# Attention in a two-block layer stack: values become the stationary operand, and the softmax reciprocals are transposed instead of the results

## What is computed

```
p = softmax(logits, axis=-1)                     # per head, 128 queries x 128 or 256 keys
o = einsum("bhqs,bshd->bqhd", p, v)              # head width 64
y = g_a * (o_sparse @ w_branch_a) + g_b * (o_fox @ w_branch_b)
```

## Time and profile before

| | |
|---|---|
| three runs | 1537.84, 1539.54, 1540.49 us (median 1539.54) |
| profiled execution, first to last instruction (its span) | 1539.0 us |
| instructions | 31311 |
| TensorE clock granted, mean | 0.991 of full speed |
| DMA | 290.51 MB, mean 189 GB/s |

### The profile page before, as it was taken

The page is one execution under the profiler, slowest core; times in us unless marked ns, Lnnn a source line. Parts: engine busy times, 40 slices in busy tenths (PEclk is TensorE's granted clock), DMA queues, the critical chain, the costliest instruction groups (busy, mean ns, idle before and its releaser), DMA issues.

```text
span 1539.0 us, 31311 instructions
## 1 busy us (share of the span) xinstructions
PE 1495.4 (97%) x12608; PEld 1433.2 (93%) x12608; DVE 1144.0 (74%) x2202; ACT 833.0 (54%) x1509; POOL 31.2 (2%) x36
## 2 busy tenths in 40 slices
PE   5999999999998999999999999999999999999997
PEld 3898998999997999989999999999999999999997
DVE  5758566888645587668987678878966988888774
ACT  3655545655434556446665565645455754645453
POOL 0000001000000000010001000000000000000000
PEclk8999999999999999999999999999999999999998
DMA  9655555567776452354555543443446444444430
GB/s 397 247 205 194 204 222 219 217 254 271 274 271 251 166 205 97 144 185 142 188 190 197 212 172 118 174 176 138 159 151 243 155 152 161 168 161 144 168 129 29
DMA packets 48128, 290.51 MB, mean 189 GB/s; under 512 B 10024, under 2 KB 12328, under 8 KB 13424
## 3 DMA queue, kind: packets, MB, share of 16 engines
q1 hardware_dynamic: 39168, 280.83, 48.7%
q10 hardware_dynamic: 8816, 7.67, 1.5%
HBM read 286.09 MB, written 2.39 MB: 187 GB/s over the span
## 4 chain that ended last, share of the span: by engine, by line
PE 57%; DVE 1%; ACT 1%; DMA 0%; issue 0%; DVEq 0%; ACTq 0%
PE bank L1371 17%; PE bank L1377 16%; PE bank L1372 16%; PE bank L1621 2%; PE sums L1546 1%; PE sums L1436 1%; PE bank L1410 1%; PE bank L1415 1%; PE bank L1409 1%; PE bank L1528 1%; PE bank L1519 1%; DMA mem_x<-mem_t 0%; DVE w_lo L2066 0%; ACT w_hi L1669 0%; PE bank L1553 0%
## 5 line engine op out<-in xcount | busy, mean ns | idle before, releaser
L1371 PE MATMUL bank<-h_hi,w_hi 128*128 128x256 f32 x2256 | 632.9, 288 | 6.2 <-ACT h_hi L1766 3.7
L1372 PE MATMUL bank<-h_hi,w_lo 128*128 128x256 f32 x2256 | 622.3, 283 | 0.0
L2066 DVE TENSOR_TENSOR w_lo<-ring,w_hi 128x1024 fp32r<-128x1024 f32 x436 | 523.7, 1223 | 102.6 <-ACT w_hi L1669 100.0
L1377 PE MATMUL bank<-h_lo,w_hi 128*128 128x256 f32 x2256 | 575.7, 283 | 0.0
L1669 ACT ACTIVATE w_hi<-ring 128x1024 fp32r<-128x1024 f32 x436 | 449.3, 1054 | 131.6 <-PE bank L1377 130.6
L1371 PEld LDWEIGHTS bank<-h_hi,w_hi 128*128 128x128 f32 x2256 | 432.7, 192 | 20.1 <-issue 15.1
L1372 PEld LDWEIGHTS bank<-h_hi,w_lo 128*128 128x128 f32 x2256 | 433.0, 192 | 0.6 <-issue 0.5
L1377 PEld LDWEIGHTS bank<-h_lo,w_hi 128*128 128x128 f32 x2256 | 405.0, 192 | 0.0
L1371 PE MATMUL bank<-a_hi,w_hi 128*128 128x256 f32 x352 | 99.7, 283 | 1.2 <-DVE w_lo L2066 0.9
L1377 PE MATMUL bank<-a_lo,w_hi 128*128 128x256 f32 x352 | 98.3, 279 | 0.0
L1372 PE MATMUL bank<-a_hi,w_lo 128*128 128x256 f32 x352 | 98.2, 279 | 0.0
(11 more groups left out here) (336 smaller groups left out, 2352.8 us busy)
## 6 DMA issues: line engine op xcount, KB each, us to landing
ring<-weights SPq DMA_DIRECT2D x266, 1024.0 KB, 4.9
pos_bias<-scratch ACTq DMA_DIRECT2D x4, 512.0 KB, 4.4
x<-x_t ACTq DMA_DIRECT2D x1, 1024.0 KB, 6.0
scratch<-line ACTq DMA_DIRECT2D x1, 1024.0 KB, 5.1
mem_x<-mem_t ACTq DMA_DIRECT2D x1, 1024.0 KB, 6.9
mem_second<-mem_t ACTq DMA_DIRECT2D x1, 1024.0 KB, 6.2
out_t<-x SPq DMA_DIRECT2D x4, 256.0 KB, 2.5
co<-const SPq DMA_DIRECT2D x1, 462.0 KB, 6.4
```

The costliest lines, as they stand in the source:

```text
L1371: pe.matmul(to, WH[:, b % SPLIT, o, :], hi[:, k, :], start=(i == 0), stop=False)
L1372: pe.matmul(to, WL[:, b % SPLIT, o, :], hi[:, k, :], start=False, stop=False)
L1377: last = pe.matmul(to, WH[:, b % SPLIT, o, :], lo[:, k, :], start=False, stop=(i == n - 1))
L2066: ve.tensor_tensor(WL[:, b % SPLIT], ring_half(b), WH[:, b % SPLIT].bitcast(F32), ALU.subtract).then_inc(w_lo_v, 1)
```

## The change

`pv` now takes two pairs of heads at once. The values (64 columns) are the stationary operand and the transposed probabilities (128 columns) move; the result has features on partitions, even heads in the first 64 and odd heads in the last 64 (`to[DH * odd:...]`), the two halves alternating. So no result is transposed. The reciprocals are needed with features on partitions too: a new step `rb`, placed in front of the last `pv` of each attention, has VectorE take the reciprocals, ScalarE repeat each 64 times along a row, TensorE transpose that, and ScalarE copy it back to SBUF (in its part of `pv`). `no` then multiplies `sums` by it: into `o_val` for eight heads, straight into `ypre` for four. `ot` has no part on TensorE any more, and is gone for four heads; for eight it is put on the list a little earlier, behind a gate. `probs_t` has four slots for eight heads. The exponentials of the other attention come one pair after each `tp`. `y1` and `z` wait for counters instead of banks.

```diff
     def att_out(c, mid=None, other=None):
...
+            if other:
+                exps(other, hp)
...
+        def pv(hp, rb=None):
+
+            p.add("pv", hp=hp, norms=norms, after=c["values"] if hp == 0 else [], n=p.count("pv"),
+                  tp=tps[hp:hp + 2], psb=rb, **c)
+
+        def fill():
             if mid:
                 mid.pop(0)()
...
+        tp(0)
+        tp(1)
+        fill()
+        if H == 8:
+            tp(2)
+            pv(0)
+            tp(3)
+            fill()
+        b = p.full_bank()
+        p.add("rb", ps=b, **c)
+        pv(H // 2 - 2, b)
         for f in mid:
             f()
-        p.add("no", pvs=p.counts["pv"], **c)
+        p.add("no", pvs=p.counts["pv"], ps=b, **c)
...
         f1 = att("fox", l, 1, 8, 2 * P, 1, qk, v_taken, [choosing, choosing, choosing, None], f0)
         att_out(f0, [choosing, choosing], f1)
         s0 = att("sparse", l, 0, 8, P, 0, turned_a, ev[:2])
-        att_out(f1, [gate, choosing], s0)
+        att_out(f1, [lambda: (gate(), att_turn(f0, 4)), choosing], s0)
...
         def wait_slot(engine, st):
             before = (st.n - slots_of(st)) // 2 + 1
             if before > 0:
                 engine.wait_ge(pv_done, 2 * before)
...
             def pv(st):
...
-                for e, h in enumerate(pair_heads(st.hp)):
+                for e in range(2):
                     for k in range(nk):
-                        turned = probs_of(st)[:, st.tp.n % 2, (e * nk + k) * P:(e * nk + k + 1) * P]
-                        m = pe.matmul(to[:, h * DH:h * DH + DH], turned, v(k, h), start=(k == 0), stop=(k == nk - 1))
+                        for odd, turn in enumerate(st.tp):
+                            h = pair_heads(st.hp + odd)[e]
+                            turned = probs_of(st)[:, turn.n % slots_of(st), (e * nk + k) * P:(e * nk + k + 1) * P]
+                            m = pe.matmul(to[DH * odd:DH * odd + DH, h // 2 * P:h // 2 * P + P], v(k, h), turned,
+                                          start=(k == 0), stop=(k == nk - 1))
+                            if e == 1 and k == nk - 1:
+                                m.then_inc(pv_done, 1)
 
-            def ot(st):
+            def rb(st):
                 to = claim(st.ps)
-                pe.wait_ge(o_norm, st.a + 1)
+                pe.wait_ge(recip_wide, st.a + 1)
                 for j in range(st.H // 2):
-                    m = pe.transpose(to[:, j * P:j * P + P], out_of(st)[:, st.a % 2, j * P:j * P + P], ident)
+                    m = pe.transpose(to[:, j * P:j * P + P], wide_of(st)[:, j * P:j * P + P], ident)
                 m.then_inc(ready, 1)
...
+            def rb(st):
+                act.wait_ge(recip_ready, st.a + 1)
+                if st.a:
+                    act.wait_ge(o_norm, st.a)
+                act.activation(wide_of(st)[:, 0:st.H * DH].rearrange("p (h d) -> p h d", d=DH),
+                               stats8[:, 3, st.a % 2, 0:st.H, None].broadcast_to([P, st.H, DH]),
+                               ACT.Copy).then_inc(recip_wide, 1)
+
+            def pv(st):
+                if st.psb is not None:
+                    wait_ready(act, st.psb)
+                    act.activation(wide_of(st)[:, 0:st.H * DH], bank[st.psb.bank][:, 0:st.H * DH],
+                                   ACT.Copy).then_inc(taken[st.psb.bank], 1)
...
+            def rb(st):
                 ve.wait_ge(exped, st.hs + st.H)
...
+                ve.reciprocal(stats8[:, 3, st.a % 2, 0:st.H], stats8[:, 2, st.a % 2, 0:st.H]).then_inc(recip_ready, 1)
+
+            def no(st):
+
+                wait_taken(ve, st.ps)
+                ve.wait_ge(pv_done, 2 * st.pvs)
...
+                tt(to, src, r, ALU.mult).then_inc(o_norm, 1)
```

More of the change, by code:

```diff
@@ L255, in tp @@
             state[("L", c["slot"])] = b
[L257 to L262, removed]
-            if other:
-                for i in range(2 if hp == 1 else 1):
-                    exps(other, hp if hp > 1 else i)
+            if other:
+                exps(other, hp)
[3 more added lines that the diff above has]
+        def fill():
             if mid:
                 mid.pop(0)()
[L268 to L271, removed]
+        tp(0)
[9 more added lines that the diff above has]
+        pv(H // 2 - 2, b)
         for f in mid:
             f()
-        p.add("no", pvs=p.counts["pv"], **c)
+        p.add("no", pvs=p.counts["pv"], ps=b, **c)
     def att_turn(c, base):
-        b = p.full_bank()
-        p.add("ot", ps=b, n=p.count("ot"), base=base, **c)
-        return b
+        p.add("ot", n=p.count("ot"), base=base, **c)
     def stats(after, src, tiles=None):
@@ L545, in plan2, with z @@
     hgo = [None]
-    def z(name, l, proj, after, scale):
+    def z(name, l, proj, atts, scale):
         for j in range(2):
@@ L551, in z @@
             n = p.count("z")
-            st = p.add("z", subs=proj[j], ps=b, last_ready=b.ready, name=name, j=j, l=l, n=n, after=after[j],
+            st = p.add("z", subs=proj[j], ps=b, last_ready=b.ready, name=name, j=j, l=l, n=n, atts=atts,
                        slot=2 * order.index(name) + j, scale=scale, prev=state["z"], lag=state["lag"])
@@ L1293, in logits_of, with wait_slot, slots_of, wide_of @@
             return Lb[st.slot] if st.H == 8 else Lb2[st.slot]
+        def wait_slot(engine, st):
+            before = (st.n - slots_of(st)) // 2 + 1
+            if before > 0:
+                engine.wait_ge(pv_done, 2 * before)
         def probs_of(st):
             return PT if st.H == 8 else PT2
-        def out_of(st):
-            return otm if st.H == 8 else otm2
+        def slots_of(st):
+            return 4 if st.H == 8 else 2
+        def wide_of(st):
+            return rr if st.H == 8 else rr2
         def factors(st):
@@ L1558, in y1 @@
                 if st.j == 0 and st.br == 0:
-                    for u in st.after:
-                        wait_taken(pe, u)
+                    pe.wait_ge(o_lo, st.atts)
                 linear([(to[:, 0:S], st.subs)], OH, OL, 4 * st.br)
@@ L2386, in no @@
                             ALU.add))
[L2387 to L2393, removed]
+                ve.reciprocal(stats8[:, 3, st.a % 2, 0:st.H], stats8[:, 2, st.a % 2, 0:st.H]).then_inc(recip_ready, 1)
+            def no(st):
+                wait_taken(ve, st.ps)
+                ve.wait_ge(pv_done, 2 * st.pvs)
+                n = st.H // 2
+                if st.H == 8:
+                    to = ov[:]
+                else:
+                    to = ypre[{"mem": "mem", "win": "at"}[st.name]][:, :, st.t * P:st.t * P + P]
+                src, r = sums[:, 0:n * P], wide_of(st)[:, 0:n * P]
+                if st.H == 4:
+                    src, r = (x.rearrange("p (j q) -> p j q", q=P) for x in (src, r))
+                tt(to, src, r, ALU.mult).then_inc(o_norm, 1)
             def ot(st):
-                if st.H == 4:
-                    return
                 if st.l == 0:
@@ L2646, in z @@
                     z_lo(st.prev)
-                for u in st.after:
-                    wait_taken(ve, u)
+                if st.atts:
+                    ve.wait_ge(o_norm, st.atts)
                 src = {"mem": ypre["mem"], "at": ypre["at"], "sc": sbv, "cf": cc_, "hg": hb}[st.name][:, st.j, :]
```

77 lines of the change are left out of this document (32 added, 45 removed).

## The result

The changed kernel takes 1595.23 us (median of four runs, 1593.60 to 1595.73) where the kernel before takes 1539.26 (four runs, 1537.84 to 1540.49): a ratio of 1.036, with a 95% interval of 1.0348 to 1.0373, or 56.0 us more. The profiled execution's span is 1593.9 us against 1539.0, its mean granted clock 0.977 against 0.991. I had said 1577, with 1550 to 1597 as the range. The sign and the mechanism of the waits were right; 18 us were missing, and most of them are in the term for the clock.

What follows compares the result with a forecast made beforehand. TensorE, busy 97% of the span, was taken as the bound. New waits and exponentials 15.5 (eight heads) + 30.6 (four), plus clock 3, less gains 10.0, made 39.1: 1539.0 to 1578.1, said as 1577 us; range 1550 to 1597.

Steps and rivals of the forecast that it cites:

- the term for the clock: Second block, behind the last new wait of each layer: TensorE's clock falls to the lower level, 2 x 1.5 = 3 us.
- The products: Products with the values: 0.061 us an instruction with halves alternating, 0.3 a step; -8.0 us (steps of 16), -0.6 (of 8).
- Rival (a): Products with the values: alternated halves do not overlap, every instruction takes 0.109 us, +15, so 1592; chance 0.10.
- Waits that go: Last product of layer 1's two short eight-head attentions: the 0.68 us wait for turned probabilities goes, -1.4 us.
- exponentials: Third attention of each layer, eight heads: exponentials moved ahead of ScalarE's copy delay the first product, 2 x 0.6 us.
- The new waits: TensorE waits before transposing reciprocals: eight heads 8.9 us (layer 1) and 5.4 (layer 0), four heads 30.6.
- (b): New waits: a shorter chain, no weight block or taps in front, about 1.1 us an attention: 1547; chance 0.10.
- (c): New waits: reciprocals are there when TensorE comes, only the gains stand, mean wait below 0.63 us: 1529; chance 0.06.
- the main case: Whole kernel: the summed forecast with its own uncertainties, 1562 to 1592 us, given a chance of 0.70.

Runs made afterwards that it cites:

- e5: The changed kernel with nothing moved, TensorE given 90 spare products (180 instructions) ahead of its waits for the reciprocals: 1577.76 us.
- e1: The changed kernel with VectorE's reciprocals and ScalarE's spreading moved to the start of each attention's last part, ahead of its first transposes: 1534.03 us.
- e2: As e1, but the products of the even pair of heads all come before those of the odd pair, halves not alternated: 1539.86 us.
- e8: As e7, with the reciprocal step ahead of the convolution taps for three of the four four-head attentions of a layer: 1530.31 us.
- e7: As e1, with the next attention's exponentials back where they stood before the change: 1531.34 us.

## Why the prediction was right, and where it was short

**The products.** Right. I took 0.061 us an instruction and 0.3 for entering and leaving, 1.28 for a step of 16. At full clock e5 shows 1.02 from 947.53 to 948.55, and the two transposes before it take 0.42 to the products' start where two take 0.22 by themselves: 1.22. A step of 8 takes 0.59 and the same 0.2, which is the 0.79 of the sum. Rival (a) is out: it asked for 0.109 from every instruction. The Trainium skill (TensorE: Matmul & The Clock Gate, The mechanism) lets a weight load overlap a running matmul only when the row group differs. Here all stationaries have the same 128 rows and a load still starts 0.002 us behind a matmul's start (937.755 and 937.753 in e1), 16 instructions take 1.02 us, and the measurement decides. That alternation matters in steps of 16 is shown by e2.

**Waits that go, exponentials.** Right: the wait of rows 5 is gone, and two new ones for turned probabilities, in s0 of either layer, come to 1.2 us in all (0.70 and 0.52), the figure I had put down.

**The new waits.** 44.9 predicted (14.3 with eight heads and 30.6 with four), 46.8 measured (17.5 and 29.2), so two errors of opposite sign partly cancel. Four heads, first layer, predicted and measured: a0 2.0 and 1.99; a1 3.7 and 3.67; w0 4.3 and 3.49; w1 5.3 and 5.33. Eight heads: f0 of layer 1 2.07 and 2.03, of layer 0 1.26 and 1.30; too little was charged where VectorE's weight block comes ahead of its reciprocal (f1 of layer 0, 2.55, and f1 of layer 1, 3.47, where 2.7 had been put down). Rivals (b) and (c) assumed a shorter chain, and the changed kernel does not have it. In e1 the condition of (c), a mean wait under 0.63 us, holds (1.8 over 16 is 0.11), and its 1529 is near what the early kernels take, 1534 (e1) to 1530 (e8).

**The clock: the term that failed.** I charged 2 x 1.5 = 3 us, only behind w1 of each layer, with the words "in the middle of the group a slower TensorE only uses up waiting for VectorE". Two things in that were wrong. First, the low clock comes behind more of the waits. Leaving out the start and end of the execution, the granted clock is at 0.50 for 54.6 us of the changed kernel and 10.2 of the one before; seven of the eleven stretches go with the second block's waits (of 1.99 us and more), three with waits of the first block, and one stands where the kernel before has one too. Behind w1, where I did charge 1.5 us each, the two stretches are 6.8 us long with 2.5 and 2.0 of waiting in them, by an estimate 2.2 and 2.4 us lost. Second, the middle of the group has little to hide it: between two attentions VectorE and ScalarE wait for TensorE (the 6.67 us at 987.41), so a projection at 0.21 us a matmul is 0.09 lost each time. What was absorbed is small: w0's gap is 0.65 and 0.81 us shorter in the changed kernel than in e5 with its faster TensorE, 1.5 us in all. 44.4 us more at half speed, less some 6 in which TensorE was waiting anyway (the two waits ahead of w1 alone have 4.5 of them), are by an estimate 19.2 us of lost work, less those 1.5: 17.7, where e5 measured 17.5. And e1 gives it once more: of its 61.2 us, the gaps at the 16 places are 46.5 (54.4 against 7.9, counted as for e5), its turned probabilities cost 3.2 more, so 61.2 - 46.5 + 3.2 = 17.9 is the clock. The Trainium skill (TensorE: Matmul & The Clock Gate, Terms) puts the penalty at the throttled time times the part of the clock that is withheld; by that an estimate would be 44.4 x 0.5 = 22, too high by the waiting within it and the 1.5 absorbed.

**The sum as it came out:** waits 46.8, turned probabilities 0.2 less than before (1.2 against 1.4), other waits of the table 0.2 more (weights 0.9 more, the weights' low part 0.7 less), clock 17.5, against 56.0 measured: so 8.3 is left for the gains of the products, where 8.6 was predicted. That 8.3 is a remainder and was not measured by itself. Of the 18.2 us between 1577 and the result, 14.5 are the clock and 1.9 the waits; 1.1 went when I took 1577 for 1578.1 on the ground that the eight-head waits were at their full extent; they came out longer.

**Where luck helped.** 1595.2 lies above 1592, the upper end that I gave for the main case with all its uncertainties. It is inside 1550 to 1597 only because the range was stretched to take in rival (a), and (a) was false.

## What to carry to other kernels

When a change needs a small value from a helper engine in front of the bound engine's work, price the helper's queue at that place, not the operation: 0.2 and 0.4 us of work cost up to 5.3 us here, and moving the request to where its inputs are ready made the same instructions 61 us cheaper. Then price such gaps of TensorE (here 1.3 to 5.3 us, ten of the sixteen with a low stretch) twice, once as the wait and once as work at the low clock behind it, unless the other engines are shown to be behind at that point. Look also at what the early request holds up in the helper's own queue (2.06 us of TensorE's time in e7). And try the change with its requests early before it is judged by its first form.

## What the runs showed of the hardware

- Some waits of only 2.0 us bring the granted clock down to 0.50: behind the 1.99 at 951.06 the step of 951.51, 16 instructions, takes 1.90 us instead of 1.02. Others as long do not (the 2.03 at 593.51, and 2.79 at 625.24 in the same layer). Which ones do, these runs do not tell; the seven longest waits of the changed kernel (3.32 to 5.33 us) all had it at their end or behind them.
- Filling a wait with idle work paid: 90 spare products (180 instructions) made the kernel 17.5 us faster.
- With 64 stationary columns and 128 moving, an instruction of one column half starts every 0.109 us, and one of the other half beside it, 0.007 us later. Steps of 16 instructions take 1.02 us with the halves alternating and 1.48 to 1.51 in runs of eight; steps of 8 take 0.59 alternating or in runs of four. The form before, 64 columns moving, took 0.11 an instruction.
